# Chunk inverse on one core: level masks put on the product, and the chunk's matrix as a 128x128 stationary operand with two heads on its diagonal

## The reference

```python
def step(s, inp):
    r_t, w_t, k_t, v_t, kk_t, a_t = inp
    sa = jnp.einsum("bhvk,bhk->bhv", s, -kk_t)
    s = (s * w_t[:, :, None, :] + sa[..., None] * (kk_t * a_t)[:, :, None, :]
         + v_t[..., None] * k_t[:, :, None, :])
    return s, jnp.einsum("bhvk,bhk->bhv", s, r_t)
```

## Time and profile before

| | |
|---|---|
| median of three runs | 2400.13 us |
| the profiled execution's own time | 2404.69 us |
| its span | 2402.6 us |
| PE busy | 2256.2 us (94%) |
| DVE, ACT, POOL busy | 1586.4, 1253.5, 164.9 us |
| granted PE clock, mean | 0.971 |
| chunk stage of layer 0 | about 319.5 to 461 us |
| chunk stage of layer 1 | about 1158 to 1308 us |

### The profile page before, as it was taken

One profiled execution on the slowest core, in us unless ns is written; L12 is line 12 of the kernel. 1 busy time (PEld: TensorE's weight loads), 2 busy tenths in 40 slices (PEclk: granted clock), 3 DMA queues, 4 the chain that ended last, 5 costly groups with the idle time before them and its releaser, 6 DMA issues.

```text
span 2402.6 us, 43239 instructions
## 1 busy us (share of the span) xinstructions
PE 2256.2 (94%) x17495; PEld 1709.5 (71%) x17495; DVE 1586.4 (66%) x1885; ACT 1253.5 (52%) x1490; POOL 164.9 (7%) x162
## 2 busy tenths in 40 slices
PE   5999888899999999999788899999999999999997
PEld 3445467646888885555677588888888888888886
DVE  3474556524333332775465489999989898989897
ACT  3342446413222233534464267877777777777775
POOL 0000045300000000000453000000000000000000
PEclk9999989999999999999789899999999999999998
DMA  7222610343323225221003679999999999999997
GB/s 295 70 88 70 227 65 17 102 159 105 105 88 105 88 86 219 83 79 51 11 17 110 257 276 364 359 353 358 361 347 363 347 371 350 368 343 370 333 373 268
DMA packets 237413, 504.63 MB, mean 210 GB/s; under 512 B 9959, under 2 KB 78845, under 8 KB 230237
## 3 DMA queue, kind: packets, MB, share of 16 engines
q1 hardware_dynamic: 235104, 488.44, 56.9%
q10 hardware_dynamic: 2172, 14.20, 1.6%
HBM read 492.12 MB, written 6.29 MB: 207 GB/s over the span
## 4 chain that ended last, share of the span: by engine, by line
PE 90%; DVE 3%; issue 2%; DMA 2%; ACT 1%; POOL 1%; ACTq 0%; SPq 0%; DVEq 0%; POOLq 0%
PE ps L615 18%; PE ps L616 18%; PE ps L617 18%; PE ps L705 11%; PE ps L608 7%; PE ps L919 6%; PE ps L643 2%; PE ps L957 1%; DVE tail L2140 1%; PE ps L1291 1%; PE ps L1078 1%; PE ps L1130 1%; DMA tail<-in_w_out 1%; PE ps L1257 1%; PE ps L977 1%
## 5 line engine op out<-in xcount | busy, mean ns | idle before, releaser
L2444 DVE TENSOR_TENSOR weight_parts<-front,weight_parts 128x2048 fp32r<-128x2048 f32 x336 | 767.7, 2289 | 85.2 <-ACT weight_parts L1778 81.3
L1778 ACT ACTIVATE weight_parts<-front 128x2048 fp32r<-128x2048 f32 x336 | 643.6, 1919 | 247.6 <-PE ps L617 247.5
L615 PE MATMUL ps<-weight_parts,token_parts 128*128 128x512 f32 x1344 | 534.1, 397 | 1.7 <-issue 1.7
L616 PE MATMUL ps<-weight_parts,token_parts 128*128 128x512 f32 x1344 | 524.9, 391 | 0.0
L617 PE MATMUL ps<-weight_parts,token_parts 128*128 128x512 f32 x1344 | 524.7, 390 | 0.0
L615 PEld LDWEIGHTS ps<-weight_parts,token_parts 128*128 128x128 f32 x1344 | 253.1, 188 | 55.9 <-DVE weight_parts L2444 4.6
L617 PEld LDWEIGHTS ps<-weight_parts,token_parts 128*128 128x128 f32 x1344 | 252.8, 188 | 54.8
L616 PEld LDWEIGHTS ps<-weight_parts,token_parts 128*128 128x128 f32 x1344 | 253.3, 188 | 48.8
L705 PE MATMUL ps<-front,tail 128*128 128x512 f32 (+3 forms) x704 | 280.5, 554 | 6.5 <-ACT front L1458 4.4
L705 PEld LDWEIGHTS ps<-front,tail 128*128 128x128 f32 (+1 forms) x704 | 131.7, 189 | 146.2 <-issue 137.6
L919 PE MATMUL ps<-tail 64*64 64x64 f32 (+1 forms) x6976 | 171.3, 236 | 55.8 <-DVE tail L2140 22.4
(11 more groups left out here) (289 smaller groups left out, 2376.5 us busy)
## 6 DMA issues: line engine op xcount, KB each, us to landing
front<-in_exp_w SPq DMA_DIRECT2D x345, 1024.0 KB, 5.8
tail<-in_ffn_w SPq DMA_DIRECT2D x30, 1024.0 KB, 5.1
tail<-in_ada_w SPq DMA_DIRECT2D x27, 1024.0 KB, 8.6
tail<-in_w_in SPq DMA_DIRECT2D x24, 1024.0 KB, 5.1
front<-in_ada_w SPq DMA_DIRECT2D x21, 1024.0 KB, 11.3
tail<-in_w_out SPq DMA_DIRECT2D x8, 1024.0 KB, 7.7
parked_x<-front ACTq DMA_DIRECT2D x2, 2048.0 KB, 11.0
tail<-front SPq DMA_DIRECT2D x32, 128.0 KB, 2.3
```

Of the source, the lines that this page charges most:

```text
L615: mm(view, a_hi, b_hi, start=start, stop=False)
L616: mm(view, a_lo, b_hi, start=False, stop=False)
L1778: f_(whi[k % PARTS], at(A_RING2 + (k % RING2) * SLOT2, SLOT2), ACT.Copy).then_inc(cnt["act"].sem, 1)
L2444: ins = v.tensor_tensor(wlo[k % PARTS], at(A_RING2 + (k % RING2) * SLOT2, SLOT2), whi[k % PARTS], ALU.subtract)
```

## The change

The level masks of levels 1 to 5 go from the operand to the product. POOL no longer makes six masked matrices per chunk. It makes `XT` of level 0 in place (mask, then the identity: `begun`) and writes I + N for three forms (d = 0, d = 1, and d = 1 with its halves exchanged) into `NB`, a 128x128 block per form and cc with head 0 in the upper left and head 1 in the lower right 64x64; the rest of a block stays zero from one memset. `level` is then 8 products with a 128x128 stationary operand and 64 moving columns instead of 16 of 64x64, d = 0 before d = 1, each direction waiting for its half of X only (`x_copied`), with an event after d = 0 (`t_first`). DVE multiplies each direction's product by the level's mask, which holds the diagonal (two operations of 128x256 instead of one of 128x512). In `doubled`, XT is now stationary and T1 moving (level 5 the other way round), so that the result is X: ACT copies it to X (two copies, the second after DVE's first transpose), and DVE transposes it to XT, d = 1 first. ACT gets one more pair of copies per chunk (`removal_exchanged`) and loses those of `begun`; its two copies of U's rows stand apart. In PE's order a gram stands between T and XT of levels 1 and 2, and both parts of R one place later; `gram` on DVE stands likewise: T1, gram, XT1, gram.

```diff
 def level(b, n):
-    pe.wait_ge(ev("mt_ready"), mt_no(l, n, b) + 1)
-    pe.wait_ge(ev("x_ready"), (LEVELS - 1) * (STEPS * l + n) + b)
-    small(("T", l, n, b), of(MT[mt_no(l, n, b) % N_MT]), of(X), P_T, crossed)
+    c = chunk_no(l, n)
+    if b == 1:
+        pe.wait_ge(ev("nb_straight"), c + 1)
+        pe.wait_ge(ev("x_turned"), c + 1)
+    elif b == 2:
+        pe.wait_ge(ev("nb_exchanged"), c + 1)
+    key = "T", l, n, b
+    banks.take(pe, key, P_T)
+    for d in range(2):
+        if b > 1:
+            pe.wait_ge(ev("x_copied"), 2 * ((LEVELS - 2) * c + b - 2) + d + 1)
+        form = d if b % 2 else 2 * d
+        for cc in range(CC):
+            ins = mm(psum[P_T + d][:, cc * CH:(cc + 1) * CH], NB[n % 2][:, form * CC + cc, :],
+                     X[:, d, cc, :], start=cc == 0, stop=True, skip_group_check=True)
+        if d == 0:
+            ins.then_inc(ev("t_first"), 1)
+    banks.fill(ins, key)
...
-    small(("XT", l, n, b), of(T1), of(XT[n % 2]), P_X, crossed)
+        pe.wait_ge(ev("xt_begun"), chunk_no(l, n) + 1)
+    a, x = of(XT[n % 2]), of(T1)
+    if b == LEVELS - 1:
+        a, x = x, a
+    small(("XT", l, n, b), a, x, P_X, crossed)
...
 # DVE
 def level(b, n):
-    banks.done(v.tensor_tensor(T1, pair(P_T)..., idb..., ALU.add), ("T", l, n, b))
+    for d in range(2):
+        if d == 0:
+            dve.wait_ge(ev("t_first"), (LEVELS - 1) * chunk_no(l, n) + b)
+        else:
+            banks.see(dve, key)
+        ins = v.tensor_tensor(T1[:, d], pair(P_T)[:, d].rearrange("p (b c) -> p b c", b=CC),
+                              masks[:, d, 2 + b:3 + b, :].broadcast_to([P, CC, CH]), ALU.mult)
+    banks.done(ins, key)
 def doubled(b, n):
-    v.transpose(flat(X, 0), pair(P_X)[:, 0]).then_inc(ev("x0_ready"), 1)
-    v.transpose(flat(X, 1), pair(P_X)[:, 1]).then_inc(ev("x_ready"), 1)
+    v.transpose(flat(XT[n % 2], 1), pair(P_X)[:, 1]).then_inc(ev("xt_half"), 1)
+    dve.wait_ge(ev("x_copied"), 2 * ((LEVELS - 2) * chunk_no(l, n) + b - 1) + 1)
+    banks.done(v.transpose(flat(XT[n % 2], 0), pair(P_X)[:, 0]), key)
...
 # ACT
 def doubled(b, n):
-    f_(XT[n % 2][:, 0].rearrange("p a b -> p (a b)"), pair(P_X)[:, 0], ACT.Copy)
-    act.wait_ge(ev("x_ready"), (LEVELS - 1) * (STEPS * l + n) + b + 1)
-    banks.done(exchanged(XT[n % 2], pair(P_X)[:, 1]), ("XT", l, n, b))
+    f_(X[:, 0].rearrange("p a b -> p (a b)"), pair(P_X)[:, 0], ACT.Copy).then_inc(ev("x_copied"), 1)
+    act.wait_ge(ev("xt_half"), done)
+    f_(X[:, 1].rearrange("p a b -> p (a b)"), pair(P_X)[:, 1], ACT.Copy).then_inc(ev("x_copied"), 1)
...
 # POOL
-    g.tensor_tensor(MT[m % N_MT], N0, mk, ALU.mult).then_inc(ev("mt_ready"), 1)      # six per chunk
+    chain(g.tensor_tensor(XT[n % 2], N0[:, 0:2], mk, ALU.mult))                      # begun
+    g.tensor_tensor(xt, xt, idc..., ALU.add).then_inc(ev("xt_begun"), 1)
+    return g.tensor_tensor(NB[n % 2][halves[h], forms.start * CC:forms.stop * CC, h * CH:(h + 1) * CH],
+                           N0[halves[h], forms].rearrange("p a b c -> p (a b) c"), idc..., ALU.add)  # blocks
-    level_mask(n + 2, 0); begun(n + 2); level_mask(n + 2, 1); decayed(n); level_mask(n + 2, 2 to 5)
+    begun(n + 2); straight(n + 2); decayed(n); exchanged(n + 2)
```

More of the change, by code:

```diff
@@ L75, in constant_tables @@
         a, b = (s, q) if d == 0 else (q, s)
-        m = [a < b, a <= b] + [(a // (2 * w) == b // (2 * w)) & (a % (2 * w) < w) & (b % (2 * w) >= w)
-                               for w in (2 ** k for k in range(LEVELS))]
+        below = lambda a, b, w: (a // (2 * w) == b // (2 * w)) & (a % (2 * w) < w) & (b % (2 * w) >= w)
+        m = [a < b, a <= b, below(a, b, 1)] + [below(b, a, 2 ** k) | (a == b) for k in range(1, LEVELS)]
         for k, v in enumerate(m):
@@ L358, in hybrid_backbone @@
         XT = [both() for _ in range(2)]
-        MT = [both() for _ in range(N_MT)]
-        N0, X, XI, T1, RHS, SP = (both() for _ in range(6))
+        X, T1, RHS, SP = (both() for _ in range(4))
         S = [both() for _ in range(2)]
+        wide = lambda slots: [next(at_chunk) for _ in range(slots)][0]
+        N0 = at(wide(2), 3, CC, CH)
+        NB = [at(wide(3), 3 * CC, P) for _ in range(2)]
         vrows = at(A_V, 4, HALF)
@@ L1007, in chunks @@
                         level(1, n + 1)
+                    if pre:
+                        gram(n + 2, 0)
+                    if inv:
+                        doubled(1, n + 1)
                     if n > 0:
@@ L1021, in chunks @@
                         attention_spread(l, (0, 1))
+                    if pre:
+                        gram(n + 2, 1)
+                    if inv:
+                        doubled(2, n + 1)
                     if seq_:
@@ L1604, in out_of, with rows_of_u @@
                     copy_out(key, dst.rearrange("p a b c -> p a (b c)"), lambda _: pair(bank))
[L1606 to L1613, removed]
+                def rows_of_u(n, d):
+                    if d == 0:
+                        banks.see(act, ("U", l, n))
+                    r = halves[1 - d]
+                    ins = f_(VU[d][r].rearrange("p c h k -> p h c k"),
+                             pair(P_SEQ)[r].rearrange("p h (c k) -> p h c k", c=CC), ACT.Copy)
+                    if d:
+                        banks.done(ins, ("U", l, n))
                 def value_rows(t):
@@ L1671, in chunks @@
                 removal(0, 1)
-                begun(0)
+                removal_exchanged(0)
                 attention_root()
@@ L2220, in chunks @@
                             level(b, n + 1)
-                        if pre and b > 1:
-                            gram(n + 2, b - 2, 1)
+                        if pre and b < 3:
+                            gram(n + 2, b - 1, 0)
                         if inv:
@@ L2558, in chunks @@
-                for n in range(-2, STEPS):
+                def begun(n):
+                    c = chunk_no(l, n)
+                    pool.wait_ge(ev("n0_ready"), 2 * c + 2)
+                    if c > 1:
+                        banks.see(pool, ("U",) + two_before(l, n))
+                    mk = masks[:, :, 2, :].unsqueeze(2).broadcast_to([P, 2, CC, CH])
+                    chain(g.tensor_tensor(XT[n % 2], N0[:, 0:2], mk, ALU.mult))
+                    xt = XT[n % 2].rearrange("p a b c -> p (a b) c")
+                    g.tensor_tensor(xt, xt, idc.unsqueeze(1).broadcast_to([P, 2 * CC, CH]), ALU.add
+                                    ).then_inc(ev("xt_begun"), 1)
@@ new lines, in blocks, with block @@
+                def blocks(n, forms):
+                    def block(h):
+                        return g.tensor_tensor(NB[n % 2][halves[h], forms.start * CC:forms.stop * CC, h * CH:(h + 1) * CH],
+                                               N0[halves[h], forms].rearrange("p a b c -> p (a b) c"),
+                                               idc[halves[h]].unsqueeze(1).broadcast_to(
+                                                   [CH, (forms.stop - forms.start) * CC, CH]), ALU.add)
+                    chain(block(0))
+                    return block(1)
@@ L2559, in chunks @@
+                banks.see(pool, ("GH", l, 0, 0))
+                chain(g.memset(NB[0].rearrange("p a b -> p (a b)"), 0.0))
+                begun(0)
+                straight(0)
+                exchanged(0)
+                chain(g.memset(NB[1].rearrange("p a b -> p (a b)"), 0.0))
+                for n in range(-1, STEPS):
                     pre = n + 2 < STEPS
                     if pre:
-                        level_mask(n + 2, 0)
                         begun(n + 2)
-                        level_mask(n + 2, 1)
+                        straight(n + 2)
```

109 lines of the change are left out of this document (44 added, 65 removed).

## The result

The changed kernel takes 2495.47 us (median of four runs, 2491.63 to 2501.75), the kernel before 2399.46 us beside it: ratio 1.0405, 95% interval 1.038 to 1.043, 96 us more. The forecast was 2455 us with a range up to 2492. Direction and place were right, the size was not.

A forecast was written before the change was run, and what follows sets the result against it. The prediction took the chunk stages to be bound by one chunk's inverse chain, with PE's other products in its gaps. Its terms, 45 + 13 + 2.6 - 6, gave +55 us on 2400: 2455 us, eight-in-ten range 2405 to 2492.

The forecast's parts named there:

- The price of a T: PE's time for the new T: 16 records at 106 ns, 1.70 us instead of 0.45.
- The step that settled it: Earlier records with 128-column stationary operands: loading paces them, 106 ns on the whole array; moving fewer columns gives nothing back.
- The first rival: Faster: T's load hides behind the pass before, records take 53 ns; -26 us, 2374 us; chance 9%.
- The full iteration: One full iteration of the chunk stage: net +3.2 us over the measured 17.4.
- the walk: Stepping once through an iteration's new order by durations: 18.8 us, against 15.3 for the order before.
- The hops: Waits between products of a level: T to XT +0.9 us, XT to T -0.35; a bare level 0.55 longer.
- +13: Two filling iterations (n = -1): half of ten levels +0.6 us at full clock, half +2 at the lower clock.
- The full-clock terms: Forecast parts without the lower clock: full iterations +45, filling levels at 0.6 us each, start +2.6, POOL's waits -6.
- +45: 14 full iterations of the chunk stages, at net +3.2 us each.
- -6: PE's waits for POOL in layer 1, 6.1 us in 3 waits, all expected to vanish.
- The rival that came true in part: Slower still: PE at its lower clock inside full iterations, 1.7 us per level, +30, 2485 us; chance 14%.
- +1.3 per layer: Start of each layer: four POOL operations before T1 instead of three, 5.2 us against 3.9; +2.6 in all.

The follow-up runs named there:

- e7_t128x64: Changed kernel with T as 16 products whose stationary operand is 128 rows by 64 columns; 2392.04 us, ratio 0.9967 to the kernel before.
- e2_wide: Changed kernel with each product of T moving its 64 columns twice, second copy unused; 2455.02 us, ratio 1.0219 to the kernel before.
- e10_wide_start: Changed kernel with T's columns moved twice and four 128x512 products ahead of each layer's first T; 2449.95 us, ratio 1.0199 to the kernel before.
- e6_start_only: Changed kernel with four 128x512 products ahead of each layer's first T only; 2470.89 us, ratio 1.0297 to the kernel before.

## Why the prediction missed

**The price of a T: right.** The forecast had 106 ns per record and 1.70 us of PE; measured are 113 ns and, from T's start to the next shape's, 1.93 us. The step that settled it, L1090 and L960 of the earlier trace rows, held, and e7_t128x64 and e2_wide bear it out: rows cost nothing, and movement under the load is free. The first rival (load hidden behind the pass before) is refuted. Its pace of 53 ns, which is also the low bound, is not four times the 15 ns of the 64x64 row, which makes 60; the forecast does not hang on it.

**The full iteration: right in sum, by two errors that cancel.** Forecast +3.2 us and 20.6 us in all; measured 20.7 in layer 0 at full clock, and (495.07 - 392.48) / 5 = 20.5 over five. PE has 16215 records in all, as forecast. But the walk by itself gave 18.8. It took 1.70 for T instead of 1.93 and 0.9 for a gram instead of 1.09 (403.36 to 404.45), with five T and two grams some 1.5 us of the 1.9 that it was short per iteration, and the forecast kept 1.8 us of other waits, mostly "issue", that are no longer there: that share of the chain went from 12.3% to 1.4%. The quiet part has 18 packets of the instruction queue still, but PE hardly waits for them. That its longer products hide them is likely, and no run tested it.

**The hops: XT to T right.** 1.29 us for a forecast of 1.24.

**The filling iterations and the clock: this step failed.** The prediction put "+13" there, "half of the ten levels each way", and treated the lower clock as something that the trace of before sets: so many levels, those of the filling iterations. It even allowed that denser work would lift the clock earlier. In the changed kernel the lower level lasts through the filling iteration and most of the next one in layer 0, and to 1290 us, three iterations, in layer 1. That is 21 of the 80 T where the forecast had five. The lower clock costs some 49 us instead of the 7 that the +13 had for it (13 less ten levels of 0.6 at full clock), a term mis-sized by some 42 us. The whole forecast was 41 us short, so this term explains it, to the 10 us or so to which the split is good. The full-clock terms, 45 + 6 + 2.6 - 6 = 48, are what e10_wide_start measures, 48; to agree so closely is luck, since the +45 is right by two errors, the -6 was misread (below), and the measured figure is 44 to 54 by what it is held against, the doubled moving taken off.

**The rival that came true in part.** "PE falls to its lower clock level inside full iterations" had 14% and 2485 us, from a quarter of 70 levels. It was the right mechanism. The argument against it, that gaps get shorter, did not hold: the fourth window above has no gap at all and a clock of 0.54. Its price per level, 1.7 us, is right for T alone (3.67 against 1.97) and left out the rest: the gram and XT of such a level run at half clock too, and the level takes 7.4 us (1272.12 to 1279.54) against 4.3 at full clock (401.43 to 405.74), 3.1 more.

**POOL and the start: the "-6" was wrong.** The earlier trace rows has 6.1 us in three waits, the longest 4.3. That longest one is the wait ahead of the first T of layer 1, which the change does not take away; only 1.8 us in two waits lay inside the loop and are gone. In the changed kernel one wait of PE for POOL is left in layer 1, of 5.6 us, again the start. In layer 0 POOL's four operations and their gaps took 5.65 us, from 313.95 to T1 at 319.60 (forecast 5.2, before 4.2), so the +1.3 per layer was right. T1 of layer 0 came no later only because POOL began 1.4 us earlier there, for which no run gives the reason; T1 of layer 1 came 1.4 later (1202.71 against 1158.00, less the 43.3 us of layer 0). With 2 instead of 6 the full-clock terms give 52.

## What to carry to other kernels

Price a small float32 product by the larger of what it loads and what it moves (here 106 to 117 ns a record with 128 columns loaded and 2 to 128 moved, and 226 ns with 256 moved, 1.96 us for the 8 records of L608 at 1145.93 in the kernel before): packing two 64x64 blocks into one 128x128 operand halved the number of products and made them 4 times as dear together, because 128 columns are loaded for 64 that move. Look at the granted clock by window before and after a change, not at busy time: a PE that is busy all the time with such products can sit at half its clock (0.54 in a window of 26 us), and then every further product of that kind costs twice its time (3.67 against 1.97 us). Where a time falls when work is added, as in e2_wide, the clock is the first thing to read.

## What was not expected of the hardware

PE was at 1.2 GHz for nearly all of 26 us in which its busy time was 26.00 us, and the same iterations ran at 2.4 GHz once each of these products moved twice the columns in the same time (2.02 against 1.97 us). What the chip asks for before it grants the higher level is not settled by these runs, and neither is why the runs of e6_start_only lie 29 us apart. The runs show that the clock stayed up when each of these products moved twice as many columns; whether it is the moving, the writing of the results or something else that goes with it, they do not tell. A record with 128 rows by 64 columns ran as fast as one with 64 by 64 (30 ns, two at a time).
